# Regrouping the experts' input by selection products, with fifteen expert weight slots

## The chip, the cores and the metric

The kernel runs on one core of a Trainium2 chip. The metric is the device time in microseconds, the median of three executions. Times and rows of the profile are of one further, profiled execution.

## The reference

One inference step of a decoder layer over 288 tokens (256 of a prompt and 8 sequences of 4 sampled tokens), model width 2048, everything in 32-bit floats: a mixing block, a cross-attention into 256 memory tokens, a mixture of experts, and a last normalization. The part that matters here, cut:

```python
def hier_moe(h, wg, bg, we, be, w_gate, w_up, w_down):       # h is rmsnorm(x, norm_moe)
    t = h.reshape(-1, d)
    p_g = softmax(t @ wg + bg); g_sel = argmax(p_g)           # one of 4 groups
    ...                                                       # the best 2 of its 4 experts
    gate = sum(one_hot(expert_idx, 16) * wts)                 # 16 experts, 2 per token
    a = einsum('nd,edf->nef', t, w_gate)                      # 2048 x 512 per expert
    u = einsum('nd,edf->nef', t, w_up)
    act = silu(a) * u * gate
    out = einsum('nef,efd->nd', act, w_down)                  # 512 x 2048 per expert
```

## The kernel before

Activations lie with the width across partitions: `hT[:, b, :]` holds rows 128*b to 128*b+127 of the 2048 for all 288 tokens, `xT` the residual. Every projection before the experts reads its weights in tiles of 1 MB through a ring and works on `hT`.

The experts' weights are read in 1 MB tiles too, 12 for each expert: four pairs of a gate tile and an up tile (512 rows of the 2048 each), and four down tiles. Jobs of at most 64 tokens of one expert are worked on in pairs. A pair is 24 tiles, numbered m = 0 to 23 and on in the next pair: 0 to 7 are the first job's gate and up tiles (`branch(0, ...)`, L1176), 8 to 15 the second's (`second_branch`, L1217), 16 to 23 the down tiles of both (`down`, L1240). In this execution there are 8 pairs, 192 tiles; the first pair's branches stand ahead of the loop.

Where a tile goes is `moe_slot(m)` (L430) of 14 slots; when it may be loaded is `moe_lag(m)` (L435): tile m waits until tile m - lag has been used. The lag is 12, and 24 for the tiles m%24 = 0, 1, 12 and 13. SyncE issues all loads in this order (`moe_load`, L602); `tile_used` counts the tiles that TensorE is done with, two at a time. The first 14 tiles are loaded while `w_o`, the last projection, runs. Slots 12 and 13 are the memory of `hT`, so tiles 12 and 13 wait until `hT` has been transposed. For tile 14 and all later ones SyncE first waits for `jobs_ready` (L635), the table of jobs that VectorE makes, reads the table, and then waits by the lag.

The stage between `w_o` and the experts, about 968 to 999 us, goes so:

- TensorE: `route` makes the router's logits and the mean squares from `hT` (L1103, L1107); two small sets of products turn them by token (L1140, L1141); `turn_tokens` transposes `hT` to tokens by width (L1116).
- ScalarE: `tokens_out` scales each token by the reciprocal root in `h_rstd` as it moves the transposes to `h_tok` (L1530). TensorE turns them back (`turn_back`, L1125) with the rows of the width regrouped, 16*p + b in place of 128*b + p, as the gate and up tiles want them; ScalarE moves them to `h_moe` (L1537, L1559).
- VectorE: the top-1 and top-2 choices, up to `mask_ready` (L2091); TensorE counts places (L1160, L1164); VectorE makes `pick`, the 0/1 matrix of tokens by slots (L2099 to L2105); `number_slots` (L1171) multiplies it with the token numbers, ScalarE writes the 128 slot numbers as integers (L1545).
- The gather: each slot's token number is read into a register and one column of 128 x 16 is copied from `h_moe` to `xe`. For the first job GpSimd copies slots 0 to 23 (L749), ScalarE 24 to 47 (L1567), VectorE 48 to 63 (L2129). All three wait for the last part of `h_moe` (`h_moe_out`). A column of zeros at index 0 serves empty slots. Later jobs are gathered by GpSimd in the loop. VectorE makes the gates (L2110 to L2118) ahead of its gather and the table of jobs (L2134 to L2156) behind it.

In a branch TensorE multiplies `xe` of a job with the gate tiles into partitions 0 to 63 of a bank and with the up tiles into 64 to 127; ScalarE takes the Silu of the first (L1577), VectorE multiplies with the second (L2187), TensorE turns the result (L1201). The second branch also makes the slot numbers of the next pair (L1171). Scatter products (L1214) of the pair before stand between the groups of four products per tile.

Of the kernel before, what the change touches and what calls it, by code (L numbers as in the profile page):

```python
# [13 lines left out]
P = 128  # L14
D = 2048
# [45 lines left out]
PE_EVENTS, MOE_SLOTS = 11, 14  # L61
HC = C // 2
POOL_SLOTS, ACT_SLOTS = 24, 48
NX = NJ - NE

# [7 lines left out]
for _n, _c in (("x", 1), ("pack", 1), ("h", 3), ("x_rest", 2), ("w_in", 8), ("mem", 2), ("gates", 2),  # L73
               ("w_mid", 4), ("gates_b", 2), ("w_last", 8),
               ("w_k", 3), ("mix_stat", 1), ("states", 1), ("w_k_last", 1), ("w_out", 8), ("w_q", 8),
               ("values", 8), ("heads", 2), ("w_o", 8), ("router", 1), ("h_tok", 3), ("h_moe", 1),
               ("places", 1), ("h_moe_rest", 1), ("final_stat", 1), ("y", 3)):
    UNIT[_n] = _u
    _u += _c

EVENT, _e = {}, 0
for _n, _c in (("x", 1), ("pack", 1), ("h", 3), ("x_rest", 2), ("mem", 2), ("gates", 4), ("mix_stat", 2),
               ("states", 1), ("xattn_stat", 2), ("router", 1), ("h_tok", 1), ("logits", 1), ("h_tok_rest", 2),
               ("h_moe", 1), ("places", 1), ("counts", 1), ("h_moe_rest", 1), ("pick_0", 1), ("h_moe_sample", 1), ("moe_0", 3), ("moe", 0), ("scatter", 4), ("final_sum", 1), ("y_0", 1), ("final_stat", 1), ("y_rest", 2)):
    EVENT[_n] = _e
    _e += _c
# [49 lines left out]
def build(nc, a, o):  # L136
    ctx = ExitStack()
    with ctx:
# [24 lines left out]
        pair_sums = sb("pair_sums", [P, 4, TH])  # L163
        rbias = sb("rbias", [P, NG + NE])
# [6 lines left out]
        def cut(at, *shape):  # L171
# [79 lines left out]
        token_no, at = cut(at, 4)  # L251
        assert at <= 17088
# [16 lines left out]
        moe_slots += [hT[:, :, :].rearrange("p b n -> p (b n)")[:, n * KT * TW:(n + 1) * KT * TW] for n in range(2)]  # L269
        halves = lambda x: x.rearrange("p (j k) n -> p j k n", j=3)  # L270
# [16 lines left out]
        xattn_root, logits_in, stat_out, token_root, token_rstd_ready = map(  # L287
            sem, ("xattn_root", "logits_in", "stat_out", "token_root", "token_rstd_ready"))
# [25 lines left out]
        h_tok_out, h_moe_out, root_loaded = sem("h_tok_out"), sem("h_moe_out"), sem("root_loaded")  # L314
# [126 lines left out]
        def wait_moe_tile(pe, m, i=None):  # L441

            pe.wait_ge(moe_loaded[moe_slot(m)], plus(16 * (m // moe_lag(m) + 1), i, 16 * 24 // moe_lag(m)))
# [3 lines left out]
        first_slot_sums = bank(UNIT["places"], 2)[0:1, P:P + 2 * C]  # L447

# [10 lines left out]
        e_gate = a["expert_w_gate"][0].rearrange("e (p g k) f -> e g p k f", k=KT, p=P)  # L459
        e_up = a["expert_w_up"][0].rearrange("e (p g k) f -> e g p k f", k=KT, p=P)  # L460
# [8 lines left out]
        def tokens_of_slots(engine, p, first, n):  # L469
# [3 lines left out]
                slot_row(p, first, n), engines=[engine], min_val=0, max_val=T,  # L473
                skip_runtime_bounds_check_because="a slot's sum over the tokens holds at most one token's number, 1 to T")
# [6 lines left out]
        def _(sp):  # L481
# [175 lines left out]
        def _(pool):  # L657
# [67 lines left out]
            for name in ("w_k", "w_out", "w_q", "w_v"):  # L725
# [6 lines left out]
                           allow_small_or_imprecise_dtypes=True).then_inc(consts_set, 1)  # L732
            pool.wait_ge(consts_set, 10)
# [4 lines left out]
            nc.gpsimd.iota(token_no[:, 0:3], pattern=[[P, 3]], base=1, channel_multiplier=1,  # L738
                           allow_small_or_imprecise_dtypes=True).then_inc(tokens_numbered, 1)
            sum_matrix("w_o", 2, pause=4 * HREADY["w_o"] + 4)  # L740
            pool.wait_ge(tile_used, TILE["moe"])
            nc.gpsimd.memset(h_moe_or_zero[:, :, 0:1], 0.0).then_inc(tokens_numbered, 1)

            def gather(p, s, slots):

                for first in range(0, slots, 16):
                    at = C * s + first
                    for n, token in enumerate(tokens_of_slots(mybir.EngineType.Pool, p, at, min(16, slots - first))):
                        m = nc.gpsimd.tensor_copy(xe[:, :, at + n:at + n + 1], h_moe_or_zero[:, :, bass.ds(token, 1)])  # L749
                m.then_inc(xe_ready, 1)  # L750

            pool.wait_ge(tokens_numbered, 2)
            pool.wait_ge(h_moe_out, 3)
# [14 lines left out]
        def _(pe):  # L768
# [343 lines left out]
            def turn_tokens(c, blocks):  # L1112

                uc = UNIT["h_tok"] + c
                for b in blocks:
                    m = nc.tensor.transpose(bank(uc, b // 4)[0:own_rows[c], b % 4 * P:(b % 4 + 1) * P],  # L1116
                                            hT[:, b, c * P:c * P + own_rows[c]], ident[:, :])
                return m

            def turn_back(c, out):  # L1120

                rows = own_rows[c]
                pe.wait_ge(h_tok_out, c + 1)
                for b in range(DB):
                    m = nc.tensor.transpose(out(b), (h_tok[:, c, :] if c < 2 else h_sam[0:rows, :])[:, b * P:(b + 1) * P],  # L1125
                                            ident[0:rows, 0:rows])
                m.then_inc(unit_done, 1)
# [15 lines left out]
            for c in range(1, 3):  # L1143
                start_unit(pe, UNIT["h_tok"] + c)
                turn_tokens(c, range(DB)).then_inc(unit_done, 1)
            def turn_back_chunk(c, unit):
# [20 lines left out]
            def number_slots(out):  # L1167
# [4 lines left out]
                m.then_inc(unit_done, 1)  # L1172

# [43 lines left out]
            def second_branch(t, n, i, scattered):  # L1217
# [12 lines left out]
                pe.wait_ge(pick_ready, plus(n // 2 + 1, i, 1))  # L1230
                number_slots(slot_sums)
# [39 lines left out]
            n_loops = pe.value_load(loops[0:1, 0:1], min_val=NE // 2 - 1, max_val=NJ // 2 - 1)  # L1271
            second_branch(8, 2, None, False)
# [67 lines left out]
        def _(act):  # L1340
# [207 lines left out]
            for c in range(3):  # L1548
                tokens_out(c)
# [731 lines left out]
```

## Time and profile before

| what | us |
|---|---|
| median of three runs | 1484.23 (1480.25 to 1484.84) |
| the profiled execution | 1484.51 |
| its span, first to last instruction | 1482.8 |
| TensorE busy | 1427.7 (96%) |
| VectorE, ScalarE, GpSimd busy | 555.9, 190.1, 796.8 |
| moved by DMA | 377.07 MB, mean 254 GB/s |

The page cuts the span into 40 slices. A digit is the busy tenths of a slice, GB/s what the DMA engines moved in it:

```profile
PE   6999999999999999999999999979999999999997
DMA  8344344445654444464788744747999999999993
GB/s 256 124 161 142 107 150 129 155 145 176 208 167 162 142 166 143 146 236 191 299 318 310 248 152 154 293 189 323 421 421 422 422 422 422 422 422 422 422 422 140
```

Slice 26 (964 to 1001 us) holds the stage between `w_o` and the experts; from slice 27 on the experts' tiles stream in.

### The profile page before, as it was taken

The numbers are of one execution on the slowest core, as the hardware profiler recorded it, in microseconds if no ns is written. First come the engines' busy times: TensorE is split into PE (matmuls) and PEld (weight loads), VectorE is DVE, ScalarE is ACT, GpSimd is POOL, SyncE is SP. The second block draws the span as 40 slices with busy tenths as digits, with TensorE's granted clock in tenths as the row PEclk, the third lists the DMA queues.
The fourth block names the chain that finished last, engine by engine and source line by source line (L and its number), as shares of the span: only waits on it lengthen the run. The fifth ranks groups of instructions, "written<-read, shape, count | busy, mean of one in ns | idle before, by whom it ended". The sixth has DMA issues, their size and how long they took to land.

```text
span 1482.8 us, 25563 instructions
## 1 busy us (share of the span) xinstructions
PE 1427.7 (96%) x9308; PEld 1089.8 (73%) x9308; DVE 555.9 (37%) x1067; ACT 190.1 (13%) x392; POOL 796.8 (54%) x1453
## 2 busy tenths in 40 slices
PE   6999999999999999999999999979999999999997
PEld 6999999998889999998777799963334334344344
DVE  3546578829575342222111342151112122122123
ACT  5100321000000010003222200051000000000003
POOL 3777587979987757763444467512451440522500
PEclk8999999999999999999999999989999999999999
DMA  8344344445654444464788744747999999999993
GB/s 256 124 161 142 107 150 129 155 145 176 208 167 162 142 166 143 146 236 191 299 318 310 248 152 154 293 189 323 421 421 422 422 422 422 422 422 422 422 422 140
DMA packets 106120, 377.07 MB, mean 254 GB/s; under 512 B 12421, under 2 KB 12421, under 8 KB 76290
## 3 DMA queue, kind: packets, MB, share of 16 engines
q1 hardware_dynamic: 103778, 371.68, 65.8%
q10 hardware_dynamic: 2272, 4.42, 0.9%
q8 instruction: 48, 0.79, 0.2%
q14 instruction: 22, 0.18, 0.0%
HBM read 369.30 MB, written 6.77 MB: 254 GB/s over the span
## 4 chain that ended last, share of the span: by engine, by line
PE 83%; DMA 10%; DVE 3%; ACT 2%; issue 1%; SPq 1%; POOL 0%; POOLq 0%; ACTq 0%; DVEq 0%
PE ps L840 40%; PE ps L897 13%; PE ps L1184 11%; DMA tiles<-in_expert_w_up 8%; PE ps L1250 4%; PE ps L1214 3%; PE ps L966 2%; DMA tiles<-in_expert_w_down 2%; PE ps L790 1%; PE ps L1201 1%; PE ps L984 1%; PE ps L974 1%; PE ps L1005 1%; DMA A<-in_norm_final 1%; PE ps L1032 0%
## 5 line engine op out<-in xcount | busy, mean ns | idle before, releaser
L749 POOL COPY A<-A 128x16 f32 x952 | 146.1, 213 | 289.4 <-issue 289.3
L840 PE MATMUL ps<-hT,tiles 128*128 128x144 f32 x1792 | 295.3, 288 | 3.4 <-ACT A L1406 1.5
L840 PE MATMUL ps<-A,tiles 128*128 128x144 f32 x1792 | 262.0, 286 | 0.8 <-DVE A L2003 0.7
L840 PEld LDWEIGHTS ps<-hT,tiles 128*128 128x128 f32 x1792 | 251.6, 191 | 5.0 <-issue 2.6
L840 PEld LDWEIGHTS ps<-A,tiles 128*128 128x128 f32 x1792 | 237.0, 190 | 1.9 <-DVE A L2003 0.9
L702 POOL TENSOR_TENSOR tiles<-tiles 128x512 f32<-128x512 f32 x88 | 117.3, 1333 | 173.4 <-DMA tiles<-in_w_in 70.4
L840 PE MATMUL ps<-tiles 128*128 128x144 f32 x960 | 171.1, 287 | 0.0
L1184 PE MATMUL ps<-tiles,A 128*64 128x512 f32 x512 | 147.0, 601 | 13.2 <-DMA A<-in_expert_w_up 6.4
L840 PEld LDWEIGHTS ps<-tiles 128*128 128x128 f32 x960 | 140.4, 191 | 0.0
L897 PE MATMUL ps<-tiles,mT 128*128 128x256 f32 x512 | 132.9, 382 | 1.0 <-ACT kv_stage L1440 1.0
L1709 DVE COPY pair_sums<-ps 128x144 f32<-128x144 f32 x44 | 13.5, 308 | 300.4 <-PE ps L840 300.4
L707 POOL TENSOR_TENSOR tiles<-tiles 128x512 f32<-128x512 f32 x88 | 118.9, 1351 | 6.9
L705 POOL TENSOR_TENSOR tiles<-tiles 128x512 f32<-128x512 f32 x88 | 121.6, 1382 | 0.0
L704 POOL TENSOR_TENSOR tiles<-tiles 128x512 f32<-128x512 f32 x88 | 117.5, 1335 | 6.9
L1250 PE MATMUL ps<-tiles,mT 128*64 128x512 f32 x448 | 113.8, 595 | 6.6 <-DMA tiles<-in_expert_w_down 6.5
L897 PEld LDWEIGHTS ps<-tiles,mT 128*128 128x128 f32 x512 | 94.0, 190 | 18.5 <-issue 5.4
L897 PE MATMUL ps<-tiles,A 128*128 128x256 f32 x384 | 103.8, 379 | 0.0
L1184 PEld LDWEIGHTS ps<-tiles,A 128*64 128x64 f32 x512 | 43.5, 137 | 79.2 <-issue 78.8
L692 POOL TENSOR_TENSOR tiles<-tiles 128x512 f32<-128x512 f32 x32 | 45.6, 1424 | 95.7 <-DMA tiles<-in_xa_w_v 85.7
L1184 PE MATMUL ps<-A 128*64 128x512 f32 x320 | 88.4, 600 | 0.7 <-DMA A<-in_expert_w_up 0.3
L2200 DVE TENSOR_TENSOR xT<-xT,ps 128x576 f32<-128x576 f32 x56 | 42.2, 754 | 112.7 <-PE ps L1214 112.4
L1250 PEld LDWEIGHTS ps<-tiles,mT 128*64 128x64 f32 x448 | 37.0, 137 | 62.3 <-issue 62.3
(350 smaller groups left out, 1698.6 us busy)
## 6 DMA issues: line engine op xcount, KB each, us to landing
tiles<-in_expert_w_down SPq DMA_DIRECT2D x56, 1024.0 KB, 22.4
tiles<-in_w_in SPq DMA_DIRECT2D x40, 1024.0 KB, 5.1
tiles<-in_expert_w_gate SPq DMA_DIRECT2D x32, 1024.0 KB, 22.1
tiles<-in_expert_w_up SPq DMA_DIRECT2D x32, 1024.0 KB, 22.5
A<-in_expert_w_up SPq DMA_DIRECT2D x24, 1024.0 KB, 25.2
tiles<-in_xa_w_k SPq DMA_DIRECT2D x16, 1024.0 KB, 5.1
tiles<-in_w_out SPq DMA_DIRECT2D x16, 1024.0 KB, 5.1
tiles<-in_xa_w_q SPq DMA_DIRECT2D x16, 1024.0 KB, 5.1
```

The lines of the kernel that those rows point to most:

```text
L692: step.tick(tt(t1, b12, b11, ALU.subtract))
L702: step.tick(tt(s1, a21, a22, ALU.add))
L704: tt(a21, a11, a21, ALU.subtract)
L705: step.tick(tt(s2, s1, a11, ALU.subtract))
L707: tt(s4, a12, s2, ALU.subtract).then_inc(weights_summed, 1)
L749: m = nc.gpsimd.tensor_copy(xe[:, :, at + n:at + n + 1], h_moe_or_zero[:, :, bass.ds(token, 1)])
L840: return mm(one(u + mp, x, TH), w[:, kp, mp, :], rhs, start=(first and g == 0 and kp == 0), stop=(g == 3 and kp == 1), skip_group_check=True)
L897: return mm(one(u, x, TW // 2), own, w[:, kp, :], start=(first and g == 0 and kp == 0), stop=(g == 3 and kp == 1), skip_group_check=True)
L1184: m = mm(ps[C * n:C * n + C, BRANCH_BANK + s, :], xe[:, b, C * s:C * s + C], moe_tile(t + 2 * g + n).rearrange("p (k n) -> p k n", k=KT)[: ...
L1214: m = mm(ps[:, 2 * (u % 2) + n, 0:T], y_pair[:, j * P:(j + 1) * P], spread[:, :], start=True, stop=True)
L1250: m = mm(ps[C * s:C * s + C, b, :], actT[:, s, k, :], moe_tile(16 + 2 * k + s)[:, b * TW:(b + 1) * TW], start=(k == 0), stop=(k == KT - 1))
L2200: tt(x, x, ps[:, 2 * (u % 2):2 * (u % 2) + 2, 0:T], ALU.add).then_inc(residual_added, 1)
```

## The change

- The token turns are gone. TensorE regroups the rows of `hT` straight into `h_rows` by products with `row_select`, 128 x 32 columns of the identity: `pick_rows(n)`, n = 0 to 7, is 8 products with 288 columns, and ScalarE moves each n out of PSUM in one copy of 2 x 288. The rows of the gate and up tiles are regrouped otherwise for it, which makes such a tile one stretch of memory (`"e (g p k) f"` in place of `"e (p g k) f"`); before, each partition's 8 KB lay 32 KB apart.
- The copies are unscaled. The reciprocal root comes in later: as the scale of the Silu, taken for each slot from `slot_root` (`take_roots`: 6 products with one column per pair, and `roots_out` on ScalarE), and as a factor in the gate for the linear branch.
- An empty slot now copies token 0; the column of zeros is gone.
- VectorE's gather stands ahead of the gates and the counts; the shares of the first job are 20, 24 and 20 slots in place of 24, 24 and 16.
- `keep_running(3, n)` adds products of the identity with a loaded weight tile, 128 x 512, into an otherwise unused bank: 3, 1 and 4 of them in the stage.
- There is a fifteenth weight slot. The lags become 14 for m%24 from 15 on, 10 for m%24 = 1 to 9, and 24 for m%24 = 0 and 10 to 14. Tiles 12 and 13 wait for the row moves, tile 14 for the end of `w_o`.

```diff
-PE_EVENTS, MOE_SLOTS = 11, 14
+PE_EVENTS, MOE_SLOTS, REUSE = 11, 15, 14
 HC = C // 2
-POOL_SLOTS, ACT_SLOTS = 24, 48
+POOL_SLOTS, ACT_SLOTS = 20, 44
...
-        h_sam, _ = cut(at, D)
+        slot_root, at = cut(at, 2)
         silu, at = cut(at, TW)
         act_nat, at = cut(at, TW)
-        actT, at = cut(at, 2, KT, C)
-        assert at <= DB * NM
+        assert at <= DB * NM - KT * TW
+        attention_slot, _ = cut(DB * NM - KT * TW, KT * TW)
...
-        h_moe_or_zero, at = cut(0, DB, 1 + T)
-        h_moe = h_moe_or_zero[:, :, 1:1 + T]
-        h_tok, _ = cut(at, 2, D)
+        h_rows, at = cut(0, DB, T)
...
         def moe_slot(m):
 
-            m %= 24
-            return m if m in (12, 13) else m % 12
+            return m % 24 if m % 24 < MOE_SLOTS else m % 24 - REUSE
+
+        def moe_uses(m):
+            return 2 if MOE_SLOTS <= moe_slot(m) + REUSE < 24 else 1
 
         def moe_lag(m):
-            return 24 if m % 12 < 2 else 12
+
+            return REUSE if m % 24 >= MOE_SLOTS else 24 - REUSE if moe_uses(m) == 2 else 24
...
         def wait_moe_tile(pe, m, i=None):
...
         w_in, w_out, w_q, w_k, w_v, w_o = (tiles_of(a[n][0]) for n in (
             "w_in", "w_out", "xa_w_q", "xa_w_k", "xa_w_v", "xa_w_o"))
-        e_gate = a["expert_w_gate"][0].rearrange("e (p g k) f -> e g p k f", k=KT, p=P)
-        e_up = a["expert_w_up"][0].rearrange("e (p g k) f -> e g p k f", k=KT, p=P)
+        e_gate = a["expert_w_gate"][0].rearrange("e (g p k) f -> e g p k f", k=KT, p=P)
+        e_up = a["expert_w_up"][0].rearrange("e (g p k) f -> e g p k f", k=KT, p=P)
...
                 if m >= MOE_SLOTS:
                     sp.wait_ge(tile_used, plus(TILE["moe"] + m - moe_lag(m) + 1, i, 24))
+                elif m >= 14:
+                    sp.wait_ge(tile_used, TILE["moe"])
                 elif m >= 12:
-                    after_event(sp, EVENT["h_tok_rest"] + 1)
+                    after_event(sp, EVENT["router"])
+                    sp.wait_ge(rows_moved, 2 * KT)
                 elif m < 5:
...
                     at = C * s + first
                     for n, token in enumerate(tokens_of_slots(mybir.EngineType.Pool, p, at, min(16, slots - first))):
...
             start_unit(pe, u)
-            for g in range(3):
-                route(g)
-            start_unit(pe, UNIT["h_tok"])
-            turn_tokens(0, range(12))
-            route(3).then_inc(unit_done, 1)
-            turn_tokens(0, range(12, 16)).then_inc(unit_done, 1)
+            for g in range(4):
+                m = route(g)
...
+            def keep_running(b, times):
+
+                for n in range(times):
+                    wait_moe_tile(pe, n // KT)
+                    mm(ps[:, b, :], ident[:, :], moe_tile(n // KT)[:, n % KT * TW:(n % KT + 1) * TW], start=True, stop=True)
+
+            def pick_rows(n):
+
+                if n >= 2:
+                    pe.wait_ge(rows_moved, n - 1)
+                for b in range(2):
+                    for old in range(KT):
+                        m = mm(ps[P // KT * old:P // KT * (old + 1), 6 * (n % 2) + b, 0:T], row_select[:, 2 * (n % 2) + b, :],
+                               hT[:, KT * (n // 2) + old, :], start=True, stop=True)
+                m.then_inc(rows_picked, 1)
...
@@ -1140,18 +1148,13 @@
                 mm(bank(u, 2)[:, 32 * c:32 * c + NG + NE], own, same_logit[:, :], start=True, stop=True)
                 m = mm(bank(u, 2)[:, 32 * c + 20:32 * c + 21], stat_sum[:, c * P:(c + 1) * P], ones[:, 0:1], start=True, stop=True)
             m.then_inc(unit_done, 1)
-            for c in range(1, 3):
...
-                start_unit(pe, unit)
-                turn_back(c, lambda b: bank(unit, b // 4)[:, b % 4 * P:(b % 4 + 1) * P])
-
-            turn_back_chunk(0, UNIT["h_moe"])
+            for n in range(1, 2 * KT):
+                pick_rows(n)
+            keep_running(3, WARM and WARM - 1)
+            pe.wait_ge(rows_moved, 2 * KT)
             u = UNIT["places"]
             start_unit(pe, u)
-            pe.wait_ge(consts_set, 11)
+            pe.wait_ge(consts_set, 12)
             pe.wait_ge(mask_ready, 1)
...
                 m.then_inc(unit_done, 1)
+
+            def take_roots(out):
+
+                for s in range(2):
+                    for c in range(3):
+                        n = own_rows[c]
+                        m = mm(out[:, s:s + 1], pick[0:n, c, C * s:C * s + C], h_rstd[0:n, c:c + 1], start=(c == 0), stop=(c == 2))
+                return m
+
+            keep_running(3, WARM and 1)
+            pe.wait_ge(tokens_numbered, 1)
+            pe.wait_ge(pick_ready, 1)
+            number_slots(first_slot_sums)
...
+                take_roots(slot_roots)
...
-            turn_back_chunk(1, UNIT["h_moe_rest"])
-            pe.wait_ge(tokens_numbered, 1)
-            pe.wait_ge(pick_ready, 1)
-            number_slots(first_slot_sums)
-            turn_back(2, lambda b: bank(UNIT["places"], 0)[:, b * NB * ST:(b + 1) * NB * ST])
-            read_out(pe, UNIT["h_moe_rest"])
-            read_out(pe, UNIT["places"])
-            pe.wait_ge(h_moe_out, 3)
+            keep_running(3, WARM)
+            take_roots(first_slot_roots).then_inc(unit_done, 1)
...
+            act.wait_ge(rows_moved, 2 * KT)
...
                     at = C * s + first
                     for n, token in enumerate(tokens_of_slots(mybir.EngineType.Activation, 0, at, n_slots)):
-                        m = copy(xe[:, :, at + n:at + n + 1], h_moe_or_zero[:, :, bass.ds(token, 1)])
+                        m = copy(xe[:, :, at + n:at + n + 1], h_rows[:, :, bass.ds(token, 1)])
...
                 return dst.rearrange("p (a b) -> p a b", a=4)[:, 0:2, :], ps[:, first:first + 2, :]
...
             def place_read(e, i):
...
-            gate_branch(8, 1, None)
+            after_event(act, EVENT["root_0"])
+            roots_out(first_slot_roots)
...
+            dve.wait_ge(logits_in, 1)
+            dve.wait_ge(stat_out, 1)
+            dve.sem_inc(half_free[u % 2], 2)
+            u = UNIT["logits"]
             dve.wait_ge(token_root, 1)
...
             m.then_inc(pick_ready, 1)
+            dve.wait_ge(slots_out, 1)
+            dve.wait_ge(rows_moved, 2 * KT)
+            for first in range(ACT_SLOTS, C, 16):
+                for n, token in enumerate(tokens_of_slots(mybir.EngineType.DVE, 0, first, min(16, C - first))):
+                    at = first + n
+                    m = v.tensor_copy(xe[:, :, at:at + 1], h_rows[:, :, bass.ds(token, 1)])
+            m.then_inc(xe_third_part, 1)
...
+            then(tt(G(11), G(11), h_rstd[:, 0:3].unsqueeze(2).broadcast_to([P, 3, 4]), ALU.mult))
```

## Rows read from the trace of the kernel before

**Rows 1.** Waits of TensorE, 1010 to 1460 us: total us, times, longest.
```profile
PE ps L1184 <- DMA A<-in_expert_w_up: 6.7, 7, 1.3
PE ps L1250 <- DMA tiles<-in_expert_w_down: 6.5, 5, 1.3
```

**Rows 2.** Stretches: PE, PEld, DVE, ACT, POOL busy; clock, DMA share, GB/s.
```profile
996.00:1002.00 6.00, 2.77 (x8) 1.05 (x10) 5.48 (x31) 4.73 (x39) 5.30 (x35) 0.50 0.00 1
...
1199.00:1217.00 18.00, 16.66 (x81) 6.74 (x80) 2.62 (x4) 1.55 (x5) 12.25 (x80) 1.00 1.01 422
1221.00:1255.00 34.00, 33.56 (x151) 14.28 (x149) 7.51 (x18) 0.59 (x1) 3.93 (x26) 1.00 1.01 422
1452.00:1453.00 1.00, 0.94 (x6) 0.06 (x2) 0.00 (x0) 0.00 (x0) 0.00 (x0) 1.00 0.34 139
```

**Rows 3.** SyncE's loads in order of time: start, us, tile, source.
```profile
1008.03 0.35 SPq L615 DMA_DIRECT2D A<-in_expert_w_gate  x1
...
1038.38 0.33 SPq L615 DMA_DIRECT2D kv_stage<-in_expert_w_gate  x1
```

**Rows 4.** Chain that ended last: start, us, engine, line.
```profile
1090.30 13.88 PE ps L1250 x64
...
1145.98 7.04 PE ps L1250 x32
...
1454.20 3.65 PE ps L1250 x16
```

**Rows 5.** TensorE in order of time; two instructions make one product.
```profile
968.64 0.69 PE L1103 MATMUL ps<-hT,A 128*32 128x288 f32 x8
969.15 0.67 PE L1107 MATMUL ps<-A,mean_d 128*32 128x288 f32 x8
...
985.29 0.40 PE L1160 MATMUL ps<-mT,A 128*128 128x16 f32 x2 [0.31 <-ACT mT L1530]
...
986.83 0.94 PE L1164 MATMUL ps<-mT,ones 128*128 128x16 f32 x6
...
999.24 1.08 PE L1184 MATMUL ps<-tiles,A 128*64 128x512 f32 x1 [6.10 <-POOL A L749]
...
1003.80 0.59 PE L1184 MATMUL ps<-tiles,A 128*64 128x512 f32 x1
...
1031.10 0.90 PE L1171 MATMUL ps<-A 128*1 128x128 f32 x6
1032.66 1.10 PE L1201 MATMUL ps<-ident,mT 64*128 64x64 f32 x8 [0.66 <-DVE mT L2187]
```

**Rows 6.** ScalarE in order of time.
```profile
976.71 0.26 ACT L1521 ACTIVATE mT<-ps,consts 128x3 f32<-128x3 f32 x1 [1.78 <-PE ps L1141]
...
992.54 0.26 ACT L1545 CAST tiles<-ps 1x128 int32<-1x128 f32 x1
993.17 0.59 ACT L1559 COPY A<-ps 128x512 f32<-128x512 f32 x1 [0.38 <-PE ps L1125]
995.45 3.10 ACT L1567 COPY A<-A 128x16 f32 x24 [1.68 <-issue]
...
1048.65 1.12 ACT L1591 ACTIVATE A<-ps,mT 128x1024 f32<-128x1024 f32 x1 [14.13 <-PE ps L1250]
```

**Rows 7.** VectorE in order of time.
```profile
982.18 0.34 DVE L2091 TENSOR_TENSOR mT<-mT 128x16 f32<-128x16 f32 x3
...
987.61 1.07 DVE L2105 TENSOR_SCALAR A<-A,mT 128x64 f32<-128x64 f32 x6
...
990.82 0.24 DVE L2123 COPY mT<-mT 128x3 f32<-128x3 f32 x2
995.36 2.41 DVE L2129 COPY A<-A 128x16 f32 x16 [4.29 <-issue]
...
1002.03 0.23 DVE L2156 CAST expert_of<-mT 1x8 int32<-1x8 f32 x1
```

**Rows 8.** GpSimd in order of time.
```profile
995.28 3.65 POOL L749 COPY A<-A 128x16 f32 x24 [26.38 <-issue]
```

More of the change, by code:

```diff
@@ L75 @@
                ("w_k", 3), ("mix_stat", 1), ("states", 1), ("w_k_last", 1), ("w_out", 8), ("w_q", 8),
-               ("values", 8), ("heads", 2), ("w_o", 8), ("router", 1), ("h_tok", 3), ("h_moe", 1),
-               ("places", 1), ("h_moe_rest", 1), ("final_stat", 1), ("y", 3)):
+               ("values", 8), ("heads", 2), ("w_o", 8), ("router", 1), ("logits", 1),
+               ("places", 1), ("final_stat", 1), ("y", 3)):
     UNIT[_n] = _u
@@ L82 @@
 for _n, _c in (("x", 1), ("pack", 1), ("h", 3), ("x_rest", 2), ("mem", 2), ("gates", 4), ("mix_stat", 2),
-               ("states", 1), ("xattn_stat", 2), ("router", 1), ("h_tok", 1), ("logits", 1), ("h_tok_rest", 2),
-               ("h_moe", 1), ("places", 1), ("counts", 1), ("h_moe_rest", 1), ("pick_0", 1), ("h_moe_sample", 1), ("moe_0", 3), ("moe", 0), ("scatter", 4), ("final_sum", 1), ("y_0", 1), ("final_stat", 1), ("y_rest", 2)):
+               ("states", 1), ("xattn_stat", 2), ("router", 1), ("logits", 1),
+               ("places", 1), ("counts", 1), ("pick_0", 1), ("root_0", 1), ("moe_0", 3), ("moe", 0), ("scatter", 4), ("final_sum", 1), ("y_0", 1), ("final_stat", 1), ("y_rest", 2)):
     EVENT[_n] = _e
@@ L472, in tokens_of_slots @@
             _, tokens = nc.values_load_multi_w_load_instructions(
-                slot_row(p, first, n), engines=[engine], min_val=0, max_val=T,
-                skip_runtime_bounds_check_because="a slot's sum over the tokens holds at most one token's number, 1 to T")
+                slot_row(p, first, n), engines=[engine], min_val=0, max_val=T - 1,
+                skip_runtime_bounds_check_because="a slot's sum over the tokens holds at most one token's number, 0 to T - 1")
             return tokens
@@ L1110, in _ @@
             own_rows = (P, P, NB * ST)
[L1112 to L1127, printed above, removed]
-            start_unit(pe, u)
-            for g in range(3):
-                route(g)
-            start_unit(pe, UNIT["h_tok"])
-            turn_tokens(0, range(12))
-            route(3).then_inc(unit_done, 1)
-            turn_tokens(0, range(12, 16)).then_inc(unit_done, 1)
+            start_unit(pe, u)
+            for g in range(4):
+                m = route(g)
+            m.then_inc(unit_done, 1)
+            def keep_running(b, times):
[11 more added lines that the diff above has]
+            u = UNIT["logits"]
+            start_unit(pe, u)
+            pe.wait_ge(consts_set, 12)
+            pick_rows(0)
             pe.wait_ge(logits_in, 1)
@@ L1271, in _ @@
             n_loops = pe.value_load(loops[0:1, 0:1], min_val=NE // 2 - 1, max_val=NJ // 2 - 1)
+            read_out(pe, UNIT["places"])
             second_branch(8, 2, None, False)
@@ L1545, in slots_numbered, with roots_out @@
                 copy(slot_row(p, 0, 2 * C), sums).then_inc(slots_out, 1)
-            act.wait_ge(token_rstd_ready, 1)
-            for c in range(3):
-                tokens_out(c)
-            after_event(act, EVENT["h_moe"])
-            turned_back(0, UNIT["h_moe"])
+            def roots_out(roots):
+                copy(slot_root[0:C, :], roots).then_inc(slot_root_out, 1)
+            for n in range(2 * KT):
+                act.wait_ge(rows_picked, n + 1)
+                copy(h_rows[:, 2 * n:2 * n + 2, :], ps[:, 6 * (n % 2):6 * (n % 2) + 2, 0:T]).then_inc(rows_moved, 1)
             act.wait_ge(gate_in, 2)
@@ L1554, in _ @@
             fn(G(17, 1), G(16, 1), ACT.Exp).then_inc(gate_exp, 1)
-            after_event(act, EVENT["h_moe_rest"])
-            turned_back(1, UNIT["h_moe_rest"])
             slots_numbered(first_slot_sums, EVENT["pick_0"], None, 0)
-            after_event(act, EVENT["h_moe_sample"])
-            copy(h_moe[:, :, TP:T], bank(UNIT["places"], 0).rearrange("p (b n) -> p b n", b=DB)).then_inc(h_moe_out, 1)
+            act.wait_ge(rows_moved, 2 * KT)
             act.wait_ge(slots_out, 1)
-            act.wait_ge(h_moe_out, 3)
-            act.wait_ge(tokens_numbered, 2)
             for s, parts in enumerate([[(POOL_SLOTS, 16), (POOL_SLOTS + 16, ACT_SLOTS - POOL_SLOTS - 16)], [(HC, 16), (HC + 16, 16)]]):
@@ L1572, in lower, with gate_branch @@
                 return dst.rearrange("p (a b) -> p a b", a=4)[:, 0:2, :], ps[:, first:first + 2, :]
-            def gate_branch(t, s, i):
+            def gate_branch(t, s, n, i):
+                act.wait_ge(slot_root_out, plus(n, i, 1))
                 after_tile(act, TILE["moe"] + t + 7, i, 24)
-                fn(silu[0:C, :], ps[0:C, 4 + s, :], ACT.Silu).then_inc(silu_ready, 1)
+                fn(silu[0:C, :], ps[0:C, 4 + s, :], ACT.Silu, scale=slot_root[0:C, s:s + 1]).then_inc(silu_ready, 1)
             def place_read(e, i):
@@ L1600, in _ @@
                 lower_y(i)
[L1601 to L1602 removed]
+                gate_branch(24, 0, 2, i)
+                gate_branch(32, 1, 2, i)
                 slots_numbered(slot_sums, EVENT["moe"] + 7, i, i + 2)
+                act.wait_ge(silu_ready, plus(4, i, 2))
+                roots_out(slot_roots)
                 place_read(EVENT["moe"] + 10, i)
```

61 lines of the change are left out of this document (22 added, 39 removed).

## The prediction

> **What bounds the kernel now.** I read the page's 40 slices first: the experts take everything from slice 27 on, and there the DMA engines move 422 GB/s slice after slice. Over 1010 to 1460 us TensorE waits 13.2 us in all for expert tiles, spread over the pairs [rows 1], and the DMA share is 1.01 both where down tiles land and where gate and up tiles land [rows 2]. So two resources are close to each other. TensorE unhindered takes 1145.98 - 1090.30 = 55.7 us for a pair [rows 4]; a pair's 24 tiles of 1.049 MB at 422 GB/s take 24 x 2.485 = 59.6 us. The stream sets the end: its last packets move at 1452.3 us [rows 2], TensorE takes the last tiles at 1454.20 [rows 4], and 28.6 us of finish follow that the change leaves alone. Left to itself TensorE would start the eighth down at 1146.0 + 5 x 55.7 = 1424.5 and end it at 1438.4, about 19 us before it does. What ends the kernel is therefore when the stream restarts after the first tiles, whether it ever stands still, and how many tiles are left. It restarts with tile 14, issued at 1008.03 [rows 3], and never stops: 14 to 27 give it 14 x 2.485 = 34.8 us of work, and tile 28, the first that needs a down tile used, is issued at 1038.38 [rows 3].
>
> **The stage, step by step.** *Row picks.* A pick is 8 products of 288 columns with 32-column weights. `route` has the same form; a group of 8 instructions (4 products) takes 969.15 - 968.64 = 0.51 us [rows 5], so a pick takes 1.0. ScalarE's move of 576 columns lies between 0.59 us for 512 and 1.12 for 1024 [rows 6]: 0.66. With two bank pairs TensorE is the slower, 1.0 per pick. Pick 0 fits where VectorE copies the router's sums; ScalarE takes the root at 976.71 [rows 6] and the other seven picks run from 976.7 to 983.7, the last move ends at about 984.5. Then three products that keep TensorE running, each of 2 instructions of 512 columns; 32 pairs of such instructions take 13.88 us in the down [rows 4], 0.43 each, so 0.87 a product: 986.3. `mask_ready` comes at 982.52 as before [rows 7] and no longer decides: the places start at 986.3 instead of 985.29 [rows 5], 1.0 us later.
> *Slot numbers.* Places to `pick_ready` took 985.29 to 988.68 [rows 5, 7], 3.4 us: now 989.7. TensorE does the counts and one keeping product meanwhile: 986.3 + 1.54 + 0.9 + 0.87 = 989.6 [rows 5]. The slot numbers take 0.9 at full clock [rows 5] and the cast 0.26 [rows 6]: 990.9 instead of 992.80.
> *Gather.* Before, it began 1.5 us behind the last part of `h_moe` (993.76 to 995.28 [rows 6, 8]), reading registers. That move is gone and the rows are there since 984.5, so it begins at 992.4. GpSimd's 20 copies take 3.65 x 20/24 = 3.0 [rows 8], ScalarE's 24 stay at 3.1 [rows 6], VectorE's 20 take 2.41 x 20/16 = 3.0 [rows 7] and a second set of registers, up to 0.5. The last ends at 995.9, TensorE starts 0.3 behind it as before: 996.2 instead of 999.24.
> *TensorE beside it.* Four keeping products, 3.5 us, then `take_roots`, 12 instructions. The nearest rows give 0.9 per 6 [rows 5], or 1.54 for 12 [rows 5]; I take 1.5, bounds 1.0 and 3.0. 990.6 + 3.5 + 1.5 = 995.6, just before the gather ends.
> *Clock.* Before, TensorE ran at 0.50 (1.2 GHz) from 996 to 1002 us [rows 2] after its idle 6.1 us [rows 5]. The first seven of its pairs of instructions took 1003.80 - 999.24 = 4.56 us against 7 x 0.434 = 3.04: a loss of 1.5 us, which the keeping products should save. If the clock drops during the small products or the first keeping ones all the same, they end up to 1.7 us later; half of the time it will, I say, and take a start at 996.8.
> The Trainium skill (TensorE: Matmul & The Clock Gate, section Why this matters for your kernels) asks for bursts of matmuls without idle gaps between them. By that rule the first branch runs at 2.4 GHz; the trace agrees as far as the loss behind the gap goes, and no row of before shows keeping products.
>
> **The stream.** *One tile more ahead.* Tile 14 is loaded behind tiles 12 and 13, which are issued at about 984.6; all three land by 993. *Restart.* Tile 15 needs tile 1 used, at 1000.3, and the table of jobs. VectorE now gathers first: its gather ends at 995.9, gates and counts take 991.06 - 988.68 = 2.4 and one more product 0.2 (the gates stood ahead of the gather [rows 7]), the table 1002.26 - 997.77 = 4.5 [rows 7]: 1003.0. SyncE's register reads I put at 1 us, bounds 0 and 4: tile 15 is issued at 1004.0, against 1008.03 for tile 14. *The standstill.* This is where the new distances bite. Tile 26 shares a slot with tile 16, distance 10, and tile 16 is a down tile. Tiles 15 to 25 are 11 tiles, 27.3 us of work, which end 27.3 after the restart, about 3.9 us before tile 26 can be issued: that is when the first quarter of the first down is done. Before, this instant lay 1038.38 - 999.24 = 39.1 us after TensorE's start [rows 3, 5]. Less 1.5 of clock, plus `take_roots` 1.5 of which 0.66 fills an idle stretch ahead of the turn [rows 5], it is 38.4: 996.8 + 38.4 = 1035.2.
> *From there on.* Before, 1452.3 - 1008.03 = 444.3 us lie between the issue of tile 14 and the end of 178 tiles. Tiles 26 to 191 are 12 fewer: 1035.2 + 444.3 - 12 x 2.485 = 1449.7, that is 2.6 us earlier. The fifteenth slot and the earlier table are thus mostly lost in the standstill; what counts is TensorE's earlier start. A second standstill is near: tile 50 waits for tile 40 at 1035.2 + 55.7 + 1.5 = 1092.4 and the stream needs it by 1035.2 + 24 x 2.485 = 1094.8, 2.4 us to spare. From pair to pair this grows, since TensorE's pair of 57.2 us is shorter than the stream's 59.6. Tiles 39 to 47 (distance 14) wait for gate and up tiles used long before.
>
> **In the loop.** `take_roots` costs TensorE 1.5 us a pair and ScalarE a copy of some 0.2. TensorE unhindered would end its eighth down at 996.8 + 34.5 + 7 x 57.2 + 13.9 = 1445.6, before the stream's last tile: hidden. That takes what was 19 us of slack down to about 9. If the roots cost over 1.5 + 2.4 us a pair, they are the bound.
> *The other layout.* Gate and up tiles are one stretch of 1 MB now, as the down tiles were before. Both kinds went at 422 GB/s, share 1.01 [rows 2], so I give it 0. The Trainium skill (DMA: Bandwidth & Descriptors, section Latency and other measured facts) has a large loss of rate for row pitches at large powers of two and advises contiguous tiles; the smallest such pitch on it is 512 KiB. The 32 KB here pay nothing by the rows, and the sum is the same by both.
>
> **Sum.** Start 2.4 us earlier (3.0 by the gather, 0.6 given back to the clock); the way from there to the deciding load 0.7 shorter (1.5 of clock less 0.8 of roots): this load is issued 3.2 us earlier. Before, the stream still had 34.8 - (1038.38 - 1008.03) = 4.4 us of work at that load; now none: another -4.4. But the load is tile 26, not 28, so two tiles more are to come: +5.0. Net -2.6 us. Span 1480.2; the profiled execution lay 1.7 over its span, so 1481.9, and 0.3 over the median: 1481.6.
>
> **The cases.** A change under 0.3%, 4.45 us, can't be told from none here.
> *Forecast, 0.46.* The standstill at tile 26 decides, start 995.2 to 998.5: -1 to -4.2 us, 1480 to 1483.3.
> *More gain, 0.26.* TensorE starts at 994.5 or before (registers read sooner, picks closer), or its way to the first down is shorter. Each us is a us, down to where the restart decides: 1004.0 + 444.3 - 2.5 = 1445.8, -6.5 us, 1477.7. For it: the handoffs of this stage are many. Against: the issue of tile 26 would have to come 3.9 us sooner.
> *Nothing, 0.18.* TensorE starts at 999.4: clock down through the keeping products and roots, or picks that wait for ScalarE, 0.66 + 1.0 + handoffs instead of 1.0 each. Then 1035.2 + 2.6 gives 1452.3 again: 1484.2.
> *Slower, 0.10.* The hand-off of the roots stretches the end of the second branch: silu, root copy and place read stand in a row on ScalarE, and the next down waits for them. It decides from 3.9 us more per pair. At 6 more a pair is 61.7 us, 2.1 over the stream's, and the distance of 10 ties the stream to it: 7 x 2.1 - 2.6 = +12, 1496. For it: distance 10 leaves the stream 7 tiles when TensorE is late. Against: behind the last group there are 2.1 us of scatter and slot numbers that cover a silu of 0.6.
> The likeliest is 1481.6; the range of 8 in 10 runs from 1475.5 to 1487. Faster by over 0.3%: most of the second case and the edge of the first, 0.32; slower by over 0.3%: 0.11; the rest 0.57.
>
> **What would show it.** Right: a DMA share below 1 for 2 to 5 us at about 1033 to 1037 and nowhere behind; the issue of tile 26 just behind the first quarter of the first down; first branch from about 996.8 at clock 1.00; DMA waits of TensorE down from 13 us to a few. Wrong: no gap there, or one in each pair; other GB/s than 422 for gate tiles; a `take_roots` above 3 us; picks apart by 1.7 us.

## The result

The changed kernel takes 1498.84 us (median of four runs, 1497.81 to 1499.11) against 1483.86 for the kernel before: a ratio of 1.0104, 95% interval 1.0086 to 1.0122. It is 1.0% slower, where I had forecast 0.2% faster and a range up to 1487. The profiled execution took 1499.11 us, its span is 1497.4, 14.6 more than before. Of the executions reported further down, one of `e1_after_pool12` took 5247.01 us, for a reason that nothing here shows, and the ratio given there leaves it out.

Here is the page's row of what the DMA engines moved, and its rows for instruction packets (packets, MB, share of the engines). Such a packet carries a piece of an engine's program, where all others carry data:

```profile
GB/s 253 131 151 142 111 141 141 144 165 169 211 161 157 153 150 145 178 253 134 336 336 320 206 141 142 369 151 417 420 421 422 421 421 421 398 387 422 386 381 69
...
q8 instruction: 48, 0.79, 0.2%
q14 instruction: 52, 0.43, 0.1%
```

Queue 14 of the kernel before:

```profile
q14 instruction: 22, 0.18, 0.0%
```

Before, the slices held 422 to the end; now four of the last five full ones fall to 381 to 398. And queue 14 carries 52 instruction packets, where before it carried 22.

The stage before the experts went by the predicted steps, and faster. TensorE, ScalarE, VectorE and GpSimd of the kernel after in order of time:

```profile
976.11 7.00 PE L1136 MATMUL ps<-hT,row_select 128*32 128x288 f32 x112
983.03 2.84 PE L1128 MATMUL ps<-tiles,ident 128*128 128x512 f32 x6
985.71 0.29 PE L1163 MATMUL ps<-mT,A 128*128 128x16 f32 x2
...
989.97 3.70 PE L1128 MATMUL ps<-tiles,ident 128*128 128x512 f32 x8
993.60 1.12 PE L1182 MATMUL ps<-mT,A 128*64 128x1 f32 x12
995.22 0.61 PE L1200 MATMUL ps<-tiles,A 128*64 128x512 f32 x1 [0.49 <-ACT A L1559]
```
```profile
990.08 0.26 ACT L1540 CAST tiles<-ps 1x128 int32<-1x128 f32 x1 [4.64 <-PE ps L1174]
991.75 3.37 ACT L1559 COPY A<-A 128x16 f32 x24 [1.42 <-issue]
```
```profile
991.89 3.05 DVE L2113 COPY A<-A 128x16 f32 x20 [2.90 <-issue]
...
1001.24 0.15 DVE L2158 CAST expert_of<-mT 1x8 int32<-1x8 f32 x1
```
```profile
991.86 3.04 POOL L758 COPY A<-A 128x16 f32 x20 [40.56 <-issue]
```

The first branch starts at 995.22 instead of 999.24 [rows 5], with no slow start: the next pairs of instructions follow 0.45 and 0.43 us apart. The picks stand 0.97 us apart. SyncE's loads, in order of time:

```profile
1005.17 0.35 SPq L626 DMA_DIRECT2D A<-in_expert_w_up  x1
...
1033.01 0.33 SPq L626 DMA_DIRECT2D A<-in_expert_w_gate  x1
...
1214.69 0.33 SPq L626 DMA_DIRECT2D kv_stage<-in_expert_w_gate  x1
...
1277.63 0.33 SPq L626 DMA_DIRECT2D kv_stage<-in_expert_w_gate  x1
...
1340.54 0.33 SPq L626 DMA_DIRECT2D kv_stage<-in_expert_w_gate  x1
```

Tile 26 is issued at 1033.01, 5.4 us ahead of tile 28 of before [rows 3]. Up to here the new kernel leads. But the last three rows are the same tile of successive pairs (28 and every 24th on), and they lie 62.9 us apart. In the kernel before the same tile comes 59.7 us apart (59.6 in the next pair):

```profile
1267.05 0.33 SPq L615 DMA_DIRECT2D kv_stage<-in_expert_w_gate  x1
...
1326.74 0.33 SPq L615 DMA_DIRECT2D kv_stage<-in_expert_w_gate  x1
```

Where this time is, stretches of the kernel after show (PE, PEld, DVE, ACT, POOL busy; clock, DMA share, GB/s):

```profile
1200.00:1250.00 50.00, 44.29 (x211) 18.52 (x209) 7.61 (x10) 3.49 (x8) 19.64 (x128) 1.00 1.01 421
1250.00:1300.00 50.00, 45.12 (x216) 18.22 (x214) 9.22 (x20) 2.81 (x7) 19.62 (x128) 1.00 0.98 404
1300.00:1350.00 50.00, 46.64 (x225) 19.60 (x221) 9.75 (x21) 3.49 (x8) 14.72 (x96) 1.00 0.96 397
...
1460.00:1470.00 10.00, 9.47 (x46) 3.08 (x44) 0.00 (x0) 0.03 (x1) 0.00 (x0) 1.00 0.05 21
...
1272.00:1276.00 4.00, 4.00 (x21) 1.30 (x19) 0.00 (x0) 0.00 (x0) 3.31 (x22) 1.00 0.63 205
```

The rate is full at first, and TensorE waits all the same: 29.2 us on expert tiles against 14.0 before [rows 1 show the two largest]. At the end, 1460 to 1470, 21 GB/s still flow: about one sixteenth of 421 (26), so one of the 16 engines works alone. A tile is spread over all 16, and it has landed when the last share has. The trace marks the landing of each share. Before, the last share of a tile comes 1.4 us behind the eighth, from 1060 us to the end. After, it comes 2.6 us behind it at 1060 to 1090 us, then 5.9, 9.2 and 12.5 us one, two and three pairs later, and 12 to 14 us from there on; the fifteenth share is never more than 2.1 us behind. So one engine falls behind by 3.3 us a pair. Once it is 13 us late, the other fifteen stop for it, because no slot is free (1272 to 1276).

The packet records point to the cause. Before, the instruction packets on queue 14 end at 1059 us. After, five of 8 KB come in every pair from 1087.8 us on, for example at 1209.6, 1220.2, 1231.8, 1233.4 and 1238.4 and then 62.9 us later again. Each takes 0.31 us, and the data packet that starts as it ends takes 0.66 instead of 0.31. One engine thus loses 5 x (0.31 + 0.35) = 3.3 us a pair, just the 62.9 - 59.6 and just what the landings show. Three of the five come within about 9 us of GpSimd's jump back to the start of its loop (1229.3), the other two some 125 of its instructions apart.

GpSimd waits for its instructions too. In the trace's records of its sequencer a pass of the loop is 277 instructions; at each of the six jumps back from the loop's end to its start it stands still for 5.4 to 5.7 us, against 0.2 us in the kernel before. But it has nothing to do then: behind the jump at 1229.30 the next pass waits in any case for the slot numbers, which ScalarE writes at 1267.24, and none of TensorE's longer waits between 1005 and 1475 us is put down to GpSimd. So the time is lost through the loads.

### The profile page after: what moved, and what is told of

The parts are those of the page before. It is cut to its first block, busy times and chain, and to the rows that moved or that the text cites. A ratio compares the mean times of both kernels' runs of the same rounds, so it can differ in the third digit from the quotient of the medians.

```text
span 1497.4 us, 25887 instructions
## 1 busy us (share of the span) xinstructions
PE 1435.0 (96%) x9464; PEld 1092.6 (73%) x9464; DVE 554.2 (37%) x1072; ACT 186.8 (12%) x403; POOL 795.5 (53%) x1449
## 4 chain that ended last, share of the span: by engine, by line
PE 80%; DMA 12%; DVE 3%; SPq 2%; ACT 2%; issue 1%; ACTq 0%; DVEq 0%
PE ps L848 40%; PE ps L905 13%; PE ps L1200 9%; DMA tiles<-in_expert_w_up 6%; PE ps L1267 5%; DMA A<-in_expert_w_up 3%; PE ps L1230 2%; SPq L626 2%; PE ps L974 2%; DMA tiles<-in_expert_w_down 2%; PE ps L798 1%; PE ps L992 1%; PE ps L982 1%; PE ps L1217 1%; PE ps L1040 1%
## 5 line engine op out<-in xcount | busy, mean ns | idle before, releaser
L1200 PE MATMUL ps<-tiles,A 128*64 128x512 f32 x512 | 145.6, 598 | 14.7 <-DMA A<-in_expert_w_up 9.4
L1267 PE MATMUL ps<-tiles,A 128*64 128x512 f32 x320 | 85.1, 594 | 7.0 <-DMA tiles<-in_expert_w_down 7.0
L905 PEld LDWEIGHTS ps<-tiles,A 128*128 128x128 f32 x384 | 73.0, 190 | 9.9
```

Of the source, the lines that this page charges most:

```text
L905: return mm(one(u, x, TW // 2), own, w[:, kp, :], start=(first and g == 0 and kp == 0), stop=(g == 3 and kp == 1), skip_group_check=True)
L1200: m = mm(ps[C * n:C * n + C, BRANCH_BANK + s, :], xe[:, b, C * s:C * s + C], moe_tile(t + 2 * g + n).rearrange("p (k n) -> p k n", k=KT)[: ...
L1267: m = mm(ps[C * s:C * s + C, b, :], actT[:, s, k, :], moe_tile(16 + 2 * k + s)[:, b * TW:(b + 1) * TW], start=(k == 0), stop=(k == KT - 1))
```

## The experiments

Theory P, placement: a packet of 8 KB holds 128 instructions, if one is 64 bytes; the 125 instructions between two of the packets above fit that. GpSimd's expert loop has 277 instructions in both kernels. A place is an instruction's number in the program. By my count in the programs the loop starts at place 528 before and at 520 after, since GpSimd's first gather has four slots less. At 520 it would lie across four packets and be read anew in each pair, at 528 across three and stay. The rivals are L, the other layout of the gate and up tiles, and D, the distance of 10.

**e1_after_pool12**, the loop moved by 12 places:

```diff
+            for n in range(12):
+                nc.gpsimd.memset(filler[:, n:n + 1], 0.0)
             pool.wait_ge(rows_moved, 2 * KT)
             pool.wait_ge(slots_out, 1)
             gather(0, 0, POOL_SLOTS)
```

> The kernel after, with 12 small memsets (one column each of a tile of its own) on GpSimd while it is idle ahead of its first gather; they move its expert loop of 277 instructions from place 520 to 532 of its program. Theory P (placement): in the kernel after, GpSimd's loop is read anew from memory in every pair, 5 instruction packets of 8 KB, which cost one of the 16 DMA engines 0.66 us each, 3.3 us a pair; the pair takes 62.9 us in place of 59.6. Moved by 12, the loop stays resident as in the kernel before: no such packets behind about 1070 us, a pair of 59.6 us, and the span that my prediction's steps give with the start measured at 995.2: 1033.0 + 444.3 - 29.8 = 1447.5 for the stream's end, a span of 1478, time about 1479.5. Rival L (the new layout of the gate and up tiles makes one DMA engine slower): 1498.8 as it is. Rival D (distance 10 ties the stream to TensorE): 1498.8.

Measured: 1480.14 us, ratio to before 0.9976 (0.9964 to 0.9989), span 1478.3. The page's packet row and two stretches of e1:

```profile
q14 instruction: 22, 0.18, 0.0%
```
```profile
1033.00:1036.00 3.00, 3.00 (x16) 0.99 (x14) 0.00 (x0) 0.00 (x0) 2.51 (x17) 1.00 0.81 257
...
1250.00:1300.00 50.00, 47.60 (x225) 19.48 (x221) 7.62 (x10) 3.49 (x8) 19.56 (x128) 1.00 1.01 422
```

Twelve memsets in idle time make the kernel 18.7 us faster. The rate is full to the end, a pair is 59.6 us, and GpSimd's pause at the jump is 0.2 us again. L and D fall as causes of the loss. The first of the stretches is the short standstill before tile 26. Nine executions lie between 1479.03 and 1486.50 us; the tenth is the one named above.

**e2_before_pool120** puts the fault into the kernel before, with 120 memsets at the same spot:

> The kernel before, with 120 small memsets on GpSimd in the same idle stretch: its expert loop moves from place 528 to 648, which is 520 + 128, and nothing else changes. Theory P: places 128 apart are alike (an instruction packet of 8 KB is 128 instructions of 64 B), so the loop is read anew in every pair, 5 packets each: a pair of 62.9 us once the slots' look-ahead is used up, one DMA engine some 13 us behind the others, and a time of 1484 + 7 x 3.3 minus what the look-ahead hides: between 1492 and 1507, about 1500. Rivals L and D: 1484, since neither the layout nor the distances change.

Measured: 1506.20 us, ratio 1.0147 (1.0130 to 1.0163). Packets and two stretches of e2:

```profile
q14 instruction: 53, 0.43, 0.1%
```
```profile
1350.00:1400.00 50.00, 44.55 (x202) 18.75 (x202) 10.09 (x21) 2.55 (x4) 8.64 (x57) 1.00 0.99 396
...
1460.00:1470.00 10.00, 10.00 (x50) 4.55 (x49) 2.62 (x4) 1.46 (x5) 0.00 (x0) 1.00 0.07 28
```

The same signs, in a kernel that has nothing of the change, and GpSimd's pause at the jump is 5.5 to 5.6 us here. The time is 6 us over the point that I expected, at the upper end of its range. The cost agrees with the count: 31 more packets at 0.66 us are 20.5 us, the span grew by 21.7; in the kernel after, 30 packets are 19.8, and it lies 19.1 over e1.

**e3_after_old_rows** and **e4_after_pool128**:

```diff
-        e_gate = a["expert_w_gate"][0].rearrange("e (g p k) f -> e g p k f", k=KT, p=P)
+        e_gate = a["expert_w_gate"][0].rearrange("e (p g k) f -> e g p k f", k=KT, p=P)
```

> The kernel after with the gate and up tiles read in the layout of before (each partition's 8 KB lie 32 KB apart); the row moves stay, so the experts multiply with rows in the wrong order and the outputs of the experts are not the reference's. Theory P: the time stays at 1498.8, one DMA engine late, 5 instruction packets a pair. Rival L: 1480. Rival D: 1498.8.

Measured: 1499.54 us (two executions), ratio 1.0102 (1.0081 to 1.0122), 52 packets. The layout is worth nothing that shows.

> The kernel after with 128 small memsets on GpSimd: its loop moves from place 520 to 648. Theory P with a period of 128: as slow as the kernel after, 1498.8 or some us more if the memsets delay the gather, 5 instruction packets a pair. If any move of the loop mends it (the period is not 128, or the place does not matter but the memsets do): 1480.

Measured: 1498.84 us (two executions), ratio 1.0097 (1.0077 to 1.0117), 53 packets. A shift by 128 changes nothing, a shift by 12 everything.

**e11_after_pool100** and **e12_after_pool116** test the arithmetic of the place, with 100 and 116 memsets:

> The kernel after with 100 memsets: the loop at place 620. Its 277 instructions are two packets of 128 and 21 more, so they touch three packets, or four when the loop starts in the last 20 places of one. Places 520 and 648 are slow, 528 and 532 fast: the border between packets lies at 521 to 528 and 649 to 656. From 620 to the border it is 29 to 36: three packets, fast, no packets in the loop, 1480.

> The kernel after with 116 memsets: the loop at place 636, 13 to 20 ahead of the border, so that it touches four packets. Theory P in this form: slow, 5 packets a pair, about 1499. If it takes a start within a few places of the border for another reason: 1480.

Measured in one run each: 1477.64 us with 22 packets, and 1499.87 us with 53. Places 520, 636 and 648 are slow; 528, 532 and 620 are fast. That is what four packets against three gives. GpSimd's pause at the jump parts the same way: 5.4 to 5.9 us at the slow places, 0.2 at the fast ones. **e9_share24** takes the change as it is with the old shares:

```diff
-POOL_SLOTS, ACT_SLOTS = 20, 44
+POOL_SLOTS, ACT_SLOTS = 24, 48
```

> The kernel after with the shares of the first gather as before (24, 24 and 16 slots) and no memsets: GpSimd has four slots more of code ahead of its loop, which lies at place 528 again as in the kernel before. Theory P: the loop stays resident, no instruction packets in it, a pair of 59.6 us; the gather ends 0.6 us later than in e1 by GpSimd's 24 copies: about 1480.5. Rival (something else in the new kernel than the place): 1498.8.

Measured: 1478.64 us, ratio 0.9969 (0.9956 to 0.9981), 22 packets. The four slots of the share alone decided between slower and faster.

With the place mended the steps of the prediction can be tested. **e5_before_slots** has the slots of before in the new kernel (`MOE_SLOTS = 14`, `moe_slot` and `moe_lag` as they were, and the 12 memsets):

> The kernel of e1_after_pool12 with the slots of the kernel before: 14 slots, distance 12, and 24 for four tiles. Theory S (my prediction's step): the fifteenth slot and the earlier table are nearly lost in a standstill at tile 26. Here tile 14 is issued where tile 15 was (about 1004 to 1005), nothing stands still, and 178 tiles follow: the stream ends at 1005 + 444.3 = 1449.3, 1 to 2 us later than in e1: span 1479.5 to 1480.5, time about 1481.5. Rival: if the slot counted in full, 2.5 + 1, so 1483.7.

Measured: 1481.43 us (0.9973 to 0.9992 of before). The fifteenth slot with its distances is worth 1.3 us against e1, not 3.5; the intervals of the two overlap, so even its sign is not shown.

**e6_distance_12**, `REUSE = 12` in place of 14:

> The kernel of e1_after_pool12 with REUSE = 12 in place of 14: fifteen slots, distance 12 for nine slots, 24 for six; the first load that waits for a down tile is 28, not 26. Theory S: the standstill goes, but the stream is now bound by the issue of tile 15 behind the table of jobs (1004.2 in e1): 1004.2 + 444.3 - 2.5 = 1446.0 against 1033.4 + 444.3 - 29.8 = 1447.9 in e1: 1.9 us less, span 1476.5. Rival (no standstill in e1 worth the name): no change.

Measured: 1479.20 us (0.9959 to 0.9984). The standstill is gone, 426 GB/s between 1033 and 1036. But tile 15 was issued at 1005.54, 1.3 us later than in e1. SyncE's register reads are not the reason: they take 3.8 us in both (1001.76 to 1005.54, 1000.43 to 1004.20), and the table of jobs itself came 1.3 us later. Of 1.9 us expected 0.9 came, less than these intervals tell apart.

**e7_loads_ahead** and **e8_both**, the second with `REUSE = 12` too:

```diff
             branch_tiles(0, 0, range(8))
-            branch_tiles(1, 8, range(MOE_SLOTS - 8))
+            branch_tiles(1, 8, range(8))
+            down_tiles([0, 1], 16)
             sp.wait_ge(jobs_ready, 2)
...
             with sp.Fori(0, n_loops) as i:
-                experts = [expert(i * 2 + n) for n in range(4)]
-                branch_tiles(experts[1], 8, range(MOE_SLOTS - 8, 8), i)
-                down_tiles([experts[0], expert(i * 2 + 1)], 16, i)
-                branch_tiles(experts[2], 24, range(8), i)
-                branch_tiles(experts[3], 32, range(MOE_SLOTS - 8), i)
+                experts = [expert(i * 2 + 2), expert(i * 2 + 3)]
+                branch_tiles(experts[0], 24, range(8), i)
+                branch_tiles(experts[1], 32, range(8), i)
+                down_tiles(experts, 40, i)
```

> The kernel of e1_after_pool12 with all 24 tiles of the first pair issued without the table of jobs (the first jobs are experts 0 and 1 in any case), distances 14 and 10. Tile 15 then waits only for tile 1, near 999, 5 us sooner than in e1. Theory S: no gain at all, since tile 26 still waits for tile 16 at about 1033; the standstill grows from 0.5 to about 5 us, with a DMA share well below 1 between 1028 and 1033: 1480.1. Rival (the restart is what counts): 4 us less, 1476.

> Distance 12 and the first pair's loads ahead of the table together. Theory S: tile 15 waits for tile 3, about 1002.1, and tiles 16 and 17 for tiles 4 and 5 at 1005.6, 1 us of standing still, then none: in terms of tile 15 the stream starts at 1003.1, 1003.1 + 444.3 - 2.5 = 1444.9, 3 us less than in e1: span 1475.3, time 1477. Rival (restart alone counts): 2 us less. If the two edits merely added up as S's rival has it: 6 us less.

Measured: e7 1478.02 us (0.9947 to 0.9975), e8 1476.99 us (0.9937 to 0.9970). A load and a stretch of e7, then the same stretch of e8:

```profile
999.00 0.33 SPq L627 DMA_DIRECT2D A<-in_expert_w_up  x1
...
1034.54 0.33 SPq L627 DMA_DIRECT2D A<-in_expert_w_gate  x1
```
```profile
1030.00:1033.00 3.00, 3.00 (x12) 0.96 (x10) 0.00 (x0) 0.00 (x0) 2.48 (x18) 0.63 0.01 3
```
```profile
1030.00:1033.00 3.00, 3.00 (x16) 1.04 (x14) 0.00 (x0) 0.00 (x0) 2.49 (x18) 1.00 1.03 429
```

In e7 the stream restarts at 999.0, 5.2 us sooner than in e1, and stands still before tile 26, as theory S says. Its profile shows no gain (1481.07 us, and the spans below say why); the timed median is 2.1 us under e1's, with intervals that overlap, so the claim of no gain at all is not settled by the times. e8 has no standstill and the lowest median of the kernels run, 6.5 us under that of before in the same session (1483.45) and 3.2 under e1, where 3 was expected. Its interval overlaps those of e1 and e7, so the ranking among the three is not shown.

**e10_no_keeping**, `WARM = 0`:

> The kernel of e1_after_pool12 without the eight products that keep TensorE running (WARM = 0). The places start 2.6 us sooner, bound then by mask_ready and the last row move (984.5); slot numbers and gather come about 2.5 us sooner, but TensorE idles some 3 us ahead of the first branch and runs it at 1.2 GHz for a while, 1.5 us lost as before. Theory K (the keeping products earn their place): the first branch ends later than in e1, 1 to 2 us slower, 1481.5. Rival (they delay the gather by more than they save): 1 us faster, 1479.

Measured: 1479.12 us (0.9954 to 0.9982), against 1480.14 with the keeping products. The profile shows what the clock costs, TensorE in order of time:

```profile
994.23 1.09 PE L1203 MATMUL ps<-tiles,A 128*64 128x512 f32 x1 [3.56 <-ACT A L1562]
...
998.52 0.90 PE L1203 MATMUL ps<-tiles,A 128*64 128x512 f32 x1
...
999.26 0.59 PE L1203 MATMUL ps<-tiles,A 128*64 128x512 f32 x1
```

The way from ScalarE's last row move to the first branch is 10.3 us (983.94 to 994.23) against 11.4 in e1 (982.84 to 994.25), so 1.1 us were won, not 2.5. The branch then runs its first pairs of instructions 0.86 us apart, as before, and reaches its end 2.4 us later than in e1, as theory K says. But the times do not follow: that execution took 1484.21 us, the others 1478.19 to 1480.81. Whether the keeping products pay can't be told from these runs.

The profiles of these kernels show one thing more, and it bears on theory S. The first down, up to the issue of tile 26, in e1 and in e10 (products, then the load):

```profile
1028.22 5.01 PE L1270 MATMUL ps<-A 128*64 128x512 f32 x16 [0.80 <-DVE A L2186]
1033.42 0.33 SPq L627 DMA_DIRECT2D A<-in_expert_w_gate  x1
```
```profile
1030.61 6.65 PE L1270 MATMUL ps<-A 128*64 128x512 f32 x16 [0.79 <-DVE A L2186]
1037.45 0.33 SPq L627 DMA_DIRECT2D A<-in_expert_w_gate  x1
```

The same 16 instructions take 3.65 us in the kernel after and in e9, where the granted clock is 1.00; between 1028 and 1032 us it is 0.62 in e1 and 0.60 in e7, and between 1032 and 1036 it is 0.50 in e10. Why it falls in some executions was not found. Tile 26 is issued at 1031.41 in e9, 1033.42 in e1, 1034.54 in e7 and 1037.45 in e10, and the spans are 1476.7, 1478.3, 1479.4 and 1482.5 us: 444.9 to 445.3 us behind that issue in all four, where my steps give 1480.2 - 1035.2 = 445.0. So e7, with its stream restarted 5.2 us sooner, ends 1.1 us later than e1, because its tile 26 is 1.1 us later. That is the step of the standstill, shown in the profiled executions; it may also be where a part of the scatter between executions of one kernel comes from, which no run isolates. e11, in which the stream does not stand still, ends 442.9 us behind its tile 26.

## Why the prediction was wrong

The step that failed is "From there on", the stream's term: tiles 26 to 191 at 2.485 us each, 59.6 us for a pair, taken from the kernel before as if nothing but tiles were on the engines. It measured 62.9 us a pair once the slots' look-ahead was used up, 2.62 a tile. From the issue of tile 26 to the stream's last packet I had 1449.7 - 1035.2 = 414.5 us; the kernel after took 435, e1 without the extra packets 416. The term for instruction packets was put at nothing without a reason: I counted instructions as time on their engine and never as bytes and places. The runs showed in its place five packets a pair that cost one DMA engine 3.3 us. The profile of before had a row for queue 14 with 22 packets, and I did not ask when they came. The Trainium skill (Runtime: NRT & Kernel Launch, section Instruction fetch mechanics) says that an engine's instruction memory is refilled in blocks by DMA and that a jump out of the window held there makes it fetch anew; I did not weigh it. By that rule a loop that fits in one place need not fit in another, and the runs agree. The page has the engine stand still at such a jump, and the trace agrees with 5.4 to 5.7 us of GpSimd at each. The page gives blocks of 16 KiB, where the packets of queue 14 are 8 KB and a loop on three of them stays; and it calls crossing a block mostly hidden, while here the tiles that share the DMA engine pay for it.

The other steps, with what they measured:

- Picks 1.0 us each: 0.97. Places at 986.3: 985.71. Cast ended at 990.9: 990.34. Gather from 992.4 to 995.9: 991.75 to 995.12. TensorE's start at 996.8: 995.22. Of these 1.6 us, 0.6 are my half chance of a fallen clock, which did not fall, and the rest is a gather that ended 0.8 sooner and a shorter hand-off.
- `take_roots` 1.5 us: 1.0 (1025.45 to 1026.45). Table at 1003.0: 1001.39. TensorE's pair without waits on tiles: 57.2 expected, 56.6 in e1 (tile 28 at 1036.84, its next at 1093.42). SyncE's reads 1 us: 3.8 in the kernel after and in e1, near the upper bound.
- Tile 26 at 1035.2: 1033.01. The way from TensorE's start to it 38.4: 37.8. The standstill 3.9 us: 0.4 in the kernel after and 1.2 in e1 (from 360 and 257 GB/s instead of 422 over 3 us), because both its ends were off, the restart 1.2 us late and tile 26 2.2 us early. Only e7 shows it in full.
- Layout 0: e3 shows 0. TensorE's waits on tiles, "from 13 us to a few": 29.2 in the kernel after, 9.7 in e1.
- The sum without the extra packets, 1481.6: e1 is 1480.14. In the profiled execution of e1 the span is 1.9 us under my 1480.2, and tile 26 comes 1.8 us before my 1035.2. So the mechanism named for the gain, the issue of tile 26, stands, also by the four spans above; it was not what decided.
- My slower rival (roots stretch the pair, distance 10 ties the stream) gave about the size, 7 pairs at 2 us, by luck and with the wrong cause: e1 has the roots and the distance, and is fast.

## What to carry to other kernels

Where a kernel lives on a saturated DMA stream, look at the instruction queues in the profile, and in which slices their packets come: a loop that is read anew costs the stream on one engine, and through it all 16. Before judging an edit, count whether it moves the loops of the other engines; a few instructions ahead of a loop can cost more than the edit gains, and a few idle ones can mend it. A prefetch gains only up to the first load whose slot is still in use: e7 restarted the stream 5.2 us sooner than e1, and its span still followed tile 26.

## What the hardware showed that I had not expected

- GpSimd's loop of 277 instructions stays resident at places 528, 532 and 620 and is read anew at 520, 636 and 648. That three packets stay and four do not is the reading that fits all six; how the memory is filled was not shown. Where the loop is read anew, GpSimd stands still for 5.4 to 5.9 us at each jump back.
- An instruction packet of 8 KB takes 0.31 us in the stream, and a data packet of the same size that starts as it ends 0.66 instead of 0.31. Why it doubles is open.
- 30 packets, 0.25 MB in 377, cost 19 us of 1480: the share of queue 14 is printed as 0.1%.
